# Even mixer of a three-block transformer: the value units as one 512-column operand, another order of its tiles

## The reference, cut to what matters

```python
def even_mixer(h, w_in, w_out, lam_p, subln, rope64, rope32, lambda_init, topk):
    a_q, a_k, a_v, b_q, b_k, b_v, i_q, i_k, i_w = jnp.split(h @ w_in, EVEN_SPLITS, axis=-1)
    ...
    o_a = diff_attention(a_q, a_k, a_v, lam, subln, lambda_init)
    ...
    o_b = dsa_attention(b_q, b_k, b_v, i_q, i_k, i_w, topk)
    return jnp.concatenate([o_a, o_b], axis=-1) @ w_out

# diff_attention: two softmaxes of a pair of heads are subtracted
        w = p[:, :, 0] - lam * p[:, :, 1]
        return jnp.einsum('bhqk,bkhe->bqhe', w, vf)
# dsa_attention: each query attends to the topk (64) keys of highest index score
        rel = jax.nn.relu(jnp.einsum('bqhd,bkd->bqhk', qiblk.astype(jnp.float32), kif))
        score = jnp.einsum('bqhk,bqh->bqk', rel, wiblk.astype(jnp.float32))
        ...
        _, idx = lax.top_k(score, topk)
```

## Time and profile before

| | |
|---|---|
| median of 3 runs | 1285.29 us (1285.2 to 1286.51) |
| the profiled execution | 1285.71 us |
| its span, first to last instruction | 1283.6 us |
| busy: PE, weight loads, DVE, ACT, POOL | 99%, 85%, 65%, 53%, 9% |
| granted clock of TensorE, mean | 0.999 |
| HBM | 182 GB/s over the span |

### The profile page before, as it was taken

One profiled execution on the slowest core, in us unless ns is written; L12 is line 12 of the kernel. 1 busy time (PEld: TensorE's weight loads), 2 busy tenths in 40 slices (PEclk: granted clock), 3 DMA queues, 4 the chain that ended last, 5 costly groups with the idle time before them and its releaser, 6 DMA issues.

```text
span 1283.6 us, 18274 instructions
## 1 busy us (share of the span) xinstructions
PE 1272.4 (99%) x7058; PEld 1087.9 (85%) x7058; DVE 840.6 (65%) x1114; ACT 677.0 (53%) x905; POOL 110.3 (9%) x128
## 2 busy tenths in 40 slices
PE   9999999999999999999999999999999999999998
PEld 8978888888888888887888888888888877888886
DVE  7997655565655548898765556655565776665553
ACT  6776554443544435656564444544454665564441
POOL 2771000000000000022000000000002120000000
PEclk9999999999999999999999999999999999999999
DMA  9326766563765543527565555675553755475540
GB/s 316 131 91 198 252 205 196 196 215 114 244 201 187 186 153 121 175 83 246 197 229 185 182 191 163 201 258 197 191 186 128 245 159 165 148 236 185 184 149 33
DMA packets 175054, 234.94 MB, mean 183 GB/s; under 512 B 4607, under 2 KB 154895, under 8 KB 174992
## 3 DMA queue, kind: packets, MB, share of 16 engines
q1 hardware_dynamic: 171360, 224.25, 53.1%
q0 software_dynamic: 2896, 8.65, 2.1%
q10 hardware_dynamic: 736, 1.19, 0.3%
HBM read 233.03 MB, written 1.05 MB: 182 GB/s over the span
## 4 chain that ended last, share of the span: by engine, by line
PE 93%; POOL 3%; DVE 2%; issue 1%; ACT 1%; DMA 0%; DVEq 0%; SPq 0%; POOLq 0%; ACTq 0%
PE psum L1239 23%; PE psum L1135 14%; PE psum L1137 14%; PE psum L1136 14%; PE psum L1247 12%; PE psum L1260 2%; PE psum L1202 2%; PE psum L1201 2%; PE psum L1200 2%; POOL ws L1059 2%; PE psum L1264 1%; PE psum L1471 1%; PE psum L1362 1%; PE psum L1519 1%; PE psum L1484 1%
## 5 line engine op out<-in xcount | busy, mean ns | idle before, releaser
L1910 DVE TENSOR_TENSOR w_lo<-raw,w_hi 128x2048 fp32r<-128x2048 f32 x197 | 448.9, 2284 | 83.1 <-ACT w_hi L499 81.7
L499 ACT ACTIVATE w_hi<-raw 128x2048 fp32r<-128x2048 f32 x211 | 401.4, 1906 | 30.5 <-PE psum L1137 13.7
L1239 PE MATMUL psum<-t_both,w_hi 128*128 128x512 f32 x1280 | 304.8, 390 | 0.0
L1239 PEld LDWEIGHTS psum<-t_both,w_hi 128*128 128x128 f32 x1280 | 237.4, 188 | 47.4
L1135 PE MATMUL psum<-w_hi,f_hi 128*128 128x512 f32 x488 | 192.9, 395 | 0.0
L1137 PE MATMUL psum<-w_hi,f_lo 128*128 128x512 f32 x488 | 190.2, 390 | 0.0
L1136 PE MATMUL psum<-w_lo,f_hi 128*128 128x512 f32 x488 | 190.1, 390 | 0.0
L1135 PE MATMUL psum<-w_hi,t_both 128*128 128x512 f32 (+2 forms) x464 | 165.6, 357 | 0.0
L1137 PE MATMUL psum<-w_hi,t_both 128*128 128x512 f32 (+2 forms) x464 | 162.4, 350 | 0.0
L1136 PE MATMUL psum<-w_lo,t_both 128*128 128x512 f32 (+2 forms) x464 | 162.3, 350 | 0.0
L1247 PEld LDWEIGHTS psum<-t_both,w_lo 128*128 128x128 f32 x1280 | 158.9, 192 | 3.1
(11 more groups left out here) (214 smaller groups left out, 1293.5 us busy)
## 6 DMA issues: line engine op xcount, KB each, us to landing
raw<-in_ffn_wg SPq DMA_DIRECT2D x44, 1024.0 KB, 5.6
raw<-in_ffn_wu SPq DMA_DIRECT2D x44, 1024.0 KB, 5.4
raw<-in_ffn_wd SPq DMA_DIRECT2D x44, 1024.0 KB, 5.0
raw<-in_even_w_in SPq DMA_DIRECT2D x12, 1024.0 KB, 5.2
raw<-in_odd_w_in SPq DMA_DIRECT2D x12, 1024.0 KB, 5.7
raw<-in_w_gate SPq DMA_DIRECT2D x11, 1024.0 KB, 5.5
raw<-in_w_up SPq DMA_DIRECT2D x11, 1024.0 KB, 5.5
raw<-in_w_down SPq DMA_DIRECT2D x11, 1024.0 KB, 5.0
```

Of the source, the lines that this page charges most:

```text
L499: nc.scalar.activation(w_hi[:, n % SLOTS, 0:w], raw_of(n)[:, 0:w], ACT.Copy).then_inc(hi_done, 1)
L1239: mm = nc.tensor.matmul(bank[b + c][:, :], wh[:, k, c * P:(c + 1) * P], t_both[:, k, :, :].rearrange("p a s -> p (a s)"), start=k == 0 and ...
L1910: nc.vector.tensor_tensor(w_lo[:, n % SLOTS, 0:w], raw_of(n)[:, 0:w], w_hi[:, n % SLOTS, 0:w].bitcast(F32), ALU.subtract).then_inc(lo_done, 1)
```

## The change

The two value units of group a move together ahead of the queries and keys of heads 4 to 7 and become a pair: one operand of 512 columns, in which each of the two units holds one half of the tokens (`both`). The banks 0 and 1 change places for units 4 to 13. PE's attention pieces move to other tiles: scores of the mixed pairs 2 and 3 from i = 8, 10 to 10, 12, the turns of pairs 1 to 3 from 8, 10, 12 to 8, 12, 14, and the outputs of pairs 2 and 3 from 11, 13 to 13, 15. The group's turn goes from i = 16 to 17, behind the turn of head 8, and the turn of head 9 goes inside tile 13.0 (i = 18), after two of its eight steps. The queues of ACT and DVE are written to match.

```diff
--- before.py
+++ after.py
@@ -203,11 +203,12 @@
                     return [(w, c0 + HW * t + UC * i, UC, ("rope", 64, tile_rows(t), t)) for t in range(T)]
 
                 val = lambda c0, dst, i: [(w, c0 + UC * i, UC, ("v", dst[:, :, UC * i:UC * (i + 1)]))]
+                both = lambda c0, dst: [(w, c0 + UC * i, UC, ("v", dst[:, i, :].rearrange("p (a s) -> p a s", a=2))) for i in range(T)]
                 ph["units"] = ([(w, 6 * HW, IC, ("rope", 32, iq, None)), (w, 6 * HW + IC, IC, ("tail", 32, ik, None))]
-                               + turned(0, a_qk, 0) + val(2 * HW, av, 0) + turned(0, a_qk, 1) + val(2 * HW, av, 1)
+                               + turned(0, a_qk, 0) + both(2 * HW, av) + turned(0, a_qk, 1)
                                + turned(at, b_qk, 0) + val(at + 2 * HW, bv, 0) + turned(at, b_qk, 1) + val(at + 2 * HW, bv, 1))
-                ph["bank"] = [1, 1, 0, 3] + [j % 2 for j in range(10)]
-                ph["pairs"] = [2, 5, 8, 11]
+                ph["bank"] = [1, 1, 0, 3] + [1 - j % 2 for j in range(10)]
+                ph["pairs"] = [2, 4, 6, 8, 11]
                 ph["w_out"] = a["even_w_out_2"][0]
             else:
                 q, k, v = wv(2304, 8, S), wv(4352, 8, S), wv(6400, T, D)
@@ -853,36 +854,36 @@
                 kept(2)
                 for h in range(4):
                     relu(h)
-                split_to(n0 + 9)
                 kept(3)
                 keep_unit(ph, 4)
+                split_to(n0 + 9)
                 for h in range(4, 8):
                     relu(h)
+                keep_unit(ph, 5)
                 split_to(n0 + 10)
                 exps(L, 0)
                 exps(L, 1)
-                kept(5)
                 split_to(n0 + 11)
                 keep_mixed(L, 0)
                 exps(L, 2)
                 exps(L, 3)
                 kept(6)
-                keep_unit(ph, 7)
                 split_to(n0 + 12)
                 keep_mixed(L, 1)
+                kept(7)
+                split_to(n0 + 13)
+                squares(0)
                 exps(L, 4)
                 exps(L, 5)
-                split_to(n0 + 13)
-                squares(0)
+                act.wait_ge(idx_added, 16)
+                kept(8)
+                split_to(n0 + 14)
                 keep_mixed(L, 2)
                 exps(L, 6)
                 exps(L, 7)
-                act.wait_ge(idx_added, 16)
-                kept(8)
-                split_to(n0 + 14)
-                keep_mixed(L, 3)
                 kept(9)
                 keep_unit(ph, 10)
+                keep_mixed(L, 3)
                 squares(1)
                 split_to(n0 + 15)
                 exps(L, 8)
@@ -1216,7 +1217,7 @@
                 pe.wait_ge(lo_done, n + 1)
                 finish()
 
-            def by_tokens_tile(n, b, t, width=UC, at=None):
+            def by_tokens_tile(n, b, t, width=UC, at=None, between=None):
 
                 pe.wait_ge(lo_done, n + 1)
                 wh, wl = w_cols(n, width)
@@ -1224,6 +1225,8 @@
                 at = t * UC if at is None else at
                 for k in range(KT):
                     tile_ready(t, k)
+                    if between and k == 2:
+                        between()
                     mm = three(bank[b][:, at:at + width], t_hi[:, k, ts], t_lo[:, k, ts], wh[:, k, :], wl[:, k, :], k == 0, k == KT - 1)
                 return mm
 
@@ -1556,7 +1559,7 @@
                 L, units, left = V["L"], ph["units"], ph["left"]
                 lo0 = seen[id(t_lo_ok)]
 
-                def tile(u, t):
+                def tile(u, t, between=None):
 
                     b = ph["bank"][u]
                     if t == 0:
@@ -1565,7 +1568,7 @@
                     if first:
                         mm = by_tokens_pair(n0 + first[0], b, u - first[0], ks=range(4 * t, 4 * t + 4))
                     else:
-                        mm = by_tokens_tile(n0 + u, b, t)
+                        mm = by_tokens_tile(n0 + u, b, t, between=between)
                     if t:
                         mm.then_inc(*((pair_half, 1) if u in ph["pairs"] else (unit_used, 2 if first else 1)))
 
@@ -1596,9 +1599,9 @@
                     pair_scores(L, 2 * pair)
 
                 def mixed_out(pair):
-                    if pair % 2 == 0:
-                        u = (4, 7)[pair // 2]
-                        pe.wait_ge(bank_free[ph["bank"][u]], left[u])
+                    if pair == 0:
+                        for u in (4, 5):
+                            pe.wait_ge(bank_free[ph["bank"][u]], left[u])
                     mixed_values(L, pair)
 
                 def scores(h):
@@ -1622,27 +1625,27 @@
 
                 first_four(ph, (1, 2), (0, 3), IC, lambda: turned(0), 3)
                 turned(1)
-                turned_after = {0: 2, 1: 3, 5: 5, 7: 6, 11: 8, 13: 9, 17: 11, 18: 12}
+                MIXED_SCORES, MIXED_TURN, MIXED_OUT = (4, 6, 10, 12), (6, 8, 12, 14), (7, 9, 13, 15)
+                turned_after = {0: 2, 1: 3, 7: 6, 9: 7, 11: 8, 13: 9, 17: 11, 18: 12}
                 for i in range(20):
-                    tile(4 + i // 2, i % 2)
+                    tile(4 + i // 2, i % 2, (lambda: turn(9)) if i == 18 else None)
                     if i in turned_after:
                         turned(turned_after[i])
                     if i in (1, 2):
                         index(i - 1)
-                    if i in (6, 8, 10, 12):
-                        mixed_turn(L, i // 2 - 3)
-                    if i in (4, 6, 8, 10):
-                        mixed_scores(i // 2 - 2)
-                    if i in (7, 9, 11, 13):
-                        mixed_out(i // 2 - 3)
+                    if i in MIXED_TURN:
+                        mixed_turn(L, MIXED_TURN.index(i))
+                    if i in MIXED_SCORES:
+                        mixed_scores(MIXED_SCORES.index(i))
+                    if i in MIXED_OUT:
+                        mixed_out(MIXED_OUT.index(i))
                     if i == 14:
                         scores(8)
                     if i == 16:
-                        group_turn(V["oa"][0], 6)
                         scores(10)
                         turn(8)
                     if i == 17:
-                        turn(9)
+                        group_turn(V["oa"][0], 6)
                     if i == 18:
                         values(8)
                         turn(10)
@@ -2473,8 +2476,8 @@
                 link(nc.vector.tensor_scalar(st[:, 24:25], st[:, 24:25], LAMBDA_INIT, None, ALU.subtract))
                 rope_of(0)
                 rope_of(1)
+                split_to(n0 + 6)
                 rope_of(2)
-                split_to(n0 + 6)
                 split_to(n0 + 7)
                 rope_of(3)
                 split_to(n0 + 8)
@@ -2483,33 +2486,33 @@
                 split_to(n0 + 9)
                 add_index(V, 4)
                 add_index(V, 5)
-                rope_of(5)
                 maxima(L, 0)
                 maxima(L, 1)
+                mixed(0)
+                rope_of(6)
                 add_index(V, 6)
                 add_index(V, 7)
-                mixed(0)
-                rope_of(6)
+                split_to(n0 + 10)
+                maxima(L, 2)
+                maxima(L, 3)
                 dve.wait_ge(idx_added, 16)
                 take(1)
-                maxima(L, 2)
-                maxima(L, 3)
-                split_to(n0 + 10)
                 mixed(1)
+                rope_of(7)
                 split_to(n0 + 11)
                 take(1)
+                rope_of(8)
                 maxima(L, 4)
                 maxima(L, 5)
-                rope_of(8)
+                split_to(n0 + 12)
                 mixed(2)
-                split_to(n0 + 12)
+                head_norm(0)
+                rope_of(9)
                 maxima(L, 6)
                 maxima(L, 7)
+                split_to(n0 + 13)
                 take(1)
-                rope_of(9)
                 mixed(3)
-                head_norm(0)
-                split_to(n0 + 13)
                 take(5)
                 sel = V["sel"]
                 link(nc.vector.tensor_scalar(sel, sel, TAKEN / 2, -NEG, ALU.is_le, ALU.mult))
```

## The result

The changed kernel takes 1290.03 us (median of 7 executions, 1288.62 to 1291.68); the kernel before, on the same chip, 1285.64 (7 executions, 1285.2 to 1286.51). The ratio is 1.0034, 95% interval 1.0024 to 1.0044: slower, by 4.4 us. The forecast was 1288.5 with a range of 1286.2 to 1290.8.

What follows compares the result with a forecast made beforehand. PE's own work bounds the kernel, with no slack behind DVE's selection before the turn of head 8. Saved value work, selection lag and moved turns sum to +3.2 us: 1288.5 us, range 1286.2 to 1290.8.

Steps and rivals of the forecast that it cites:

- the clock's fall: TensorE's clock falls while PE stands still near head 8's turn, adding 1.4 to 2.9 us: 1290.6 us; chance 0.16.
- The value units: Group a's value tiles: wider products save 0.4 us, joined tiles 6.1 and 7.0 save 0.13; bounds 0.3 to 0.8.
- The selection's lag: DVE's last five rounds start 2.2 us late, at 561.0, delaying the turn of head 8 to 573.5, +2.2 us.
- PE's standstill: Before head 8's turn PE idles some 3.2 us: about 0.7 before the scores of head 10, the rest for POOL.
- The moved turns: Turns of heads 9 and 10: 0.4 us wait goes, 0.1 opening added, group's turn 0.53 behind; lag becomes +3.2.
- detour: ACT's copies behind the group's turn delay head 10's exponentials and its turn, to 583.15; bounds 0 to 1.1 us.
- The sum: Whole kernel: +3.2 us on the profiled 1285.71 gives 1288.9, less 0.4 to the median: 1288.5; terms together +1.0 to +4.5.
- rival 3: TensorE's clock falls during PE's standstill near head 8's turn, adding 1.4 to 2.9 us: 1290.6 us; chance 0.16.
- That the selection is not late: DVE's idle time keeps the last five rounds at or before about 558: 1284.5 us; chance 0.10.
- that half of it is absorbed: The selection's lag is half absorbed by earlier scores 6 or a shorter ACT chain: +1.9, 1287.2 us; chance 0.16.
- Within 0.2% or slower: Whole kernel: within 2.6 us counts as no change; slower 0.66, same 0.31, faster 0.03.

Runs made afterwards that it cites:

- Combined: Changed kernel with DVE's and ACT's queues reordered and the group's turn back ahead of the scores of head 10: 1285.02 us, ratio 0.9996.
- 2 and 9 small products: Changed kernel plus unused TensorE products: 2 ahead of the scores of heads 10 and 11, 9 ahead of the turn of head 8: 1289.13 us.
- two kernels with small products: Changed kernel plus unused TensorE products in the standstills: 5 and 16 of them, 1290.1 us; 2 and 9 of them, 1289.13 us.
- both queues reordered: Changed kernel with selection rounds moved into DVE's earlier idle time, and ACT's exponentials of heads 8 and 9 ahead of squares and split: 1285.88 us.
- six rounds: Changed kernel with 6 rounds of the selection instead of 8 (48 keys per query instead of 64, another output): 1289.15 us, ratio 1.0025.
- reordered kernel before: Kernel before with ACT's exponentials of heads 8 and 9 first, head_norm(1) later and one selection round moved earlier: 1285.0 us, ratio 0.9998.
- VectorE's queue refilled: Changed kernel with all eight selection rounds kept, two of them moved into VectorE's earlier idle time: 1288.84 us, ratio 1.0023.

## Why the prediction was right, point by point

The direction, the path and the size of 3.2 us held; what the forecast had as a rival, the clock's fall, came on top of it in most executions. The forecast's own range, 1287.4 to 1289.5, does not hold the median of 1290.03. The full range does, because it took in the lower half of that rival, at a chance of 0.16; so the median came out inside it partly by luck.

- **The value units.** Forecast: four value stretches at 2.86 us, 0.53 saved with the joint. Measured: 2.86, 2.83, 2.99, and the fourth 5.70 with its neighbour. The saving is right all the same, since it goes by places and not by units: at i = 0, 1, 6 and 7 stood the narrow tiles, 2.95, 2.96, 2.94 and 2.97 us, and all four are wide now. The first two save 0.22 us; i = 5 and 6 took 2.86 and 2.94 and now 5.58 in a row, 0.22 less; i = 7 takes 2.88, 0.09 less. Combined against the kernel before shows the same half microsecond.
- **The selection's lag.** Forecast: the last rounds from 561.0, the reciprocal at 571.6, the turn of head 8 at 573.5. Measured: 560.80, 571.42, 573.27. DVE stands still 5.1 us between 516 and 555, forecast 5.5. That one round more costs its full length, and fewer rounds give back only 1 us, shows that this is the bound and that ACT's queue is the next.
- **PE's standstill.** Forecast: 3.2 us in two pieces. Measured: 0.65 and 2.32, together 2.97.
- **The moved turns.** Forecast: no wait at the turn of head 9, one of 0.5 to 1 us at that of head 10. Measured: 0.45 at head 9, which ends with ACT's copy of head 8's turn, a detour that I followed only for head 10; 0.43 at head 10. With 2 and 9 small products, the clock kept, the turn of head 10 is at 582.85, forecast 583.15. The 0.4 us taken for the wait before head 9's turn were 0.3: without a wait the rope turn and that turn lie 0.44 us apart (573.80 to 574.24 with the turn between the tiles), not 0.35.
- **The sum.** +3.2 in the span, and the two executions that keep the clock have just this. Counted from the first value tile, the turn of head 10 goes from 71.67 us to 74.86 with the small products: +3.19.
- **The clock.** A chance of 0.16 was too low: by the mean clock it fell in five of seven executions, which are 1.2 to 3.1 us longer. Only one of them has a trace: there the tile lost 1.1 us and the turn ahead of it 0.25, of 1.4 us over the two that kept it. What makes up the 3.1 of the longest is not shown; the level 1 us up that is seen at full clock too may be part of it. What I undervalued was my own: there a standstill of 2 to 3 us was enough, and the eight products of head 10's scores in the middle did not prevent it here. So the median, 1290.03, lies between forecast and rival 3 (1290.6), nearer the rival. That the fall follows from the standstill is shown by the two kernels with small products: a mean clock of 0.999 or 1.0 in all 14 executions, the tile at full speed in both traces.
- **The other rivals.** That the selection is not late, and that half of it is absorbed, are refuted by 560.80. The first was the right question all the same: with both queues reordered the selection no longer holds PE, and 1285.88 is the kernel before again.
- **Within 0.2% or slower.** 4.4 us is over the 2.6 us taken as the limit.

## What to carry to other kernels

A part that saves TensorE work pays only if every queue that meets it later stays as early as before: follow the strictly ordered queues past the moved step, and find the second bound (here ACT's exponentials behind a split) before you mend the first, since mending one alone gave 1 of 3 us. Where a new wait in TensorE is as long as those here (2.1 to 2.3 us), price the clock with it. And run the mending edit on the old kernel too: here it did as well without the change.

## What was not expected of the hardware

GpSimd hardly moves on while VectorE splits a weight unit. With six rounds POOL's four operations on heads 8 and 9 end before the split starts (574.18), and take 3.00 us, from 570.79. In the kernel before they take 5.54, with a split on DVE from 572.19 to 574.48 beside them. The last of them, which began 0.43 us ahead of the split, takes 3.43 us, while the split keeps its 2.29:

```profile
571.39 2.40 POOL L1029 TENSOR_SCALAR ws<-ws,st 128x256 f32<-128x256 f32 x3
573.76 1.41 POOL L1006 TENSOR_TENSOR st<-st,minus_half 128x4 f32<-128x4 f32 x1
```

```profile
571.76 3.43 POOL L1028 TENSOR_SCALAR ws<-ws,st 128x256 f32<-128x256 f32 x1
```

```profile
572.19 2.29 DVE L1910 TENSOR_TENSOR w_lo<-raw,w_hi 128x2048 fp32r<-128x2048 f32 x1
```

In the reordered kernel before the four take 3.31, with the split starting only at 570.63, and the operation behind them, which takes 1.04 without a split, takes 2.69:

```profile
567.84 3.31 POOL L1028 TENSOR_SCALAR ws<-ws,st 128x128 f32<-128x128 f32 x4 [8.49 <-DVE st L2199]
571.11 2.69 POOL L1005 TENSOR_TENSOR st<-st,minus_half 128x4 f32<-128x4 f32 x1
```

So a split costs POOL 2.5 us in the one case and 0.3 and 1.65 in the other. It does not always cost that much: with six rounds the same small operation starts 0.42 us ahead of the split and takes 1.41. The turn of head 8 does not depend on this, since in every case POOL's first two operations end before the split starts. What it is worth at the turn of head 9 was not separated from the order of the exponentials.

The clock can fall after PE has resumed: with six rounds PE starts again at 572.36, and the stretch 572 to 573 still has 1.00, the next 0.78, then 0.50. And a standstill of the same length lets it fall in one trace and not in another: with six rounds it fell after 2.08 us, and with VectorE's queue refilled it stayed at 1.00 after 2.09.
